# Experts of a mixture sorted by token count on chip, ten of them run with 64 slots in place of 96

## What is computed

```
def moe_ffn(h, w_router, b_router, w_up, b_up, w_down, b_down):
    logits = (t @ w_router + b_router)             # 512 tokens, 32 experts
    top_logit, top_e = lax.top_k(logits, TOP_K)    # TOP_K = 4
    gate = softmax(top_logit)
    ...
    def expert_block(args):                        # the tokens of one expert
        u = xb @ w_up[e] + b_up[e]                 # 1024 x 2048, float32
        glu = minimum(u[:, :D_FF], 7.0)
        lin = clip(u[:, D_FF:], -7.0, 7.0)
        act = glu * sigmoid(1.702 * glu) * (lin + 1.0)
        return act @ w_down[e] + b_down[e]         # 1024 x 1024, float32
    ...                                            # times gate, added per token
x = x + moe_ffn(rms_norm(x, norm_ffn_g), ...)
return rms_norm(x, norm_final_g)
```

## Time and profile before

| | |
|---|---|
| time, median of 3 runs | 1681.96 us (1681.91 to 1682.42) |
| the profiled execution | 1681.41 us, its span 1679.6 us |
| PE busy | 1625.1 us, 97% of the span |
| DVE, ACT, POOL busy | 541.3, 264.3, 211.1 us |
| read from HBM over the span | 456.51 MB |
| granted clock of PE, mean | 0.986 of full speed |

### The profile page before, as it was taken

The page is one execution under the profiler, slowest core; times in us unless marked ns, Lnnn a source line. Parts: engine busy times, 40 slices in busy tenths (PEclk is TensorE's granted clock), DMA queues, the critical chain, the costliest instruction groups (busy, mean ns, idle before and its releaser), DMA issues.

```text
span 1679.6 us, 31609 instructions
## 1 busy us (share of the span) xinstructions
PE 1625.1 (97%) x12295; PEld 743.6 (44%) x12296; DVE 541.3 (32%) x1449; ACT 264.3 (16%) x583; POOL 211.1 (13%) x205
## 2 busy tenths in 40 slices
PE   7999899999998899999999999999999999999994
PEld 3444465545545244444444444444444444444442
DVE  3224345321224523332242223322243223322232
ACT  3022333301211001110011101110011101111012
POOL 1000000150010111112111121112111121111111
PEclk9999999999998999999999999999999999999997
DMA  6211031141115799999999999999999999999995
GB/s 228 100 50 51 12 139 50 33 163 50 51 51 201 277 367 390 384 380 364 364 402 382 372 373 384 388 383 365 375 393 383 379 381 377 387 389 371 377 387 174
DMA packets 105493, 467.27 MB, mean 278 GB/s; under 512 B 14098, under 2 KB 14150, under 8 KB 72592
## 3 DMA queue, kind: packets, MB, share of 16 engines
q1 hardware_dynamic: 91768, 441.58, 66.8%
q0 software_dynamic: 13616, 25.19, 6.3%
q10 hardware_dynamic: 72, 0.02, 0.0%
HBM read 456.51 MB, written 18.87 MB: 283 GB/s over the span
## 4 chain that ended last, share of the span: by engine, by line
PE 95%; DVE 2%; ACT 1%; DMA 1%; issue 1%; ACTq 0%; POOLq 0%; POOL 0%; DVEq 0%
PE bank L735 40%; PE bank L687 23%; PE bank L763 13%; PE bank L772 6%; PE bank L724 1%; PE bank L703 1%; PE bank L713 1%; PE bank L925 1%; PE bank L908 1%; PE bank L705 1%; PE bank L716 1%; PE bank L951 1%; PE bank L750 1%; PE bank L796 1%; PE bank L852 1%
## 5 line engine op out<-in xcount | busy, mean ns | idle before, releaser
L735 PE MATMUL bank<-ring,arena 128*32 128x512 f32 x6144 | 679.3, 594 | 0.0
L735 PEld LDWEIGHTS bank<-ring,arena 128*32 128x32 f32 x6144 | 227.9, 110 | 400.0 <-issue 332.9
L763 PE MATMUL bank<-ring,arena 128*32 128x512 f32 x2048 | 267.8, 592 | 0.0
L687 PE MATMUL bank<-ring,actT 128*128 128x512 f32 x448 | 198.8, 599 | 0.1
L1579 DVE TENSOR_SCALAR tokA<-bank 64x512 f32<-64x512 f32 x64 | 43.7, 683 | 419.8 <-PE bank L735 418.7
L772 PE MATMUL bank<-ring,arena 128*32 128x512 f32 x1024 | 157.9, 592 | 0.0
L763 PEld LDWEIGHTS bank<-ring,arena 128*32 128x32 f32 x2048 | 112.9, 110 | 96.2
L593 POOL DMA_INDIRECT arena<-h_rows,arena x32 | 34.1, 1065 | 910.8 <-DVE arena L1563 853.6
L687 PEld LDWEIGHTS bank<-ring,actT 128*128 128x128 f32 x448 | 84.5, 193 | 98.8 <-issue 98.1
L1203 ACT ACTIVATE tokA<-tokA 128x512 f32<-128x512 f32 x32 | 20.1, 629 | 505.6 <-DVE tokA L1579 505.6
L687 PE MATMUL bank<-actT,ring 128*128 128x512 f32 x192 | 83.5, 593 | 0.0
(11 more groups left out here) (305 smaller groups left out, 1340.6 us busy)
## 6 DMA issues: line engine op xcount, KB each, us to landing
ring<-in_w_up SPq DMA_DIRECT2D x256, 1024.0 KB, 6.3
ring<-in_w_down SPq DMA_DIRECT2D x128, 1024.0 KB, 7.8
ring<-in_w_in SPq DMA_DIRECT2D x12, 1024.0 KB, 7.8
ring<-in_w_ck SPq DMA_DIRECT2D x4, 1024.0 KB, 6.2
ring<-in_w_out SPq DMA_DIRECT2D x4, 1024.0 KB, 6.2
ring<-in_w_cv SPq DMA_DIRECT2D x4, 1024.0 KB
ring<-in_w_cq SPq DMA_DIRECT2D x4, 1024.0 KB, 6.2
ring<-in_w_co SPq DMA_DIRECT2D x4, 1024.0 KB, 6.2
```

The costliest lines, as they stand in the source:

```text
L687: mm = pe.matmul(o, lhsT, rhs, start=(k == 0), stop=(k == KT - 1))
L735: mm = pe.matmul(bank[g][32 * t:32 * t + 32, :], lhsT, w[:, 512 * t:512 * t + 512], start=False, stop=(k == KT - 1))
L763: mm = pe.matmul(bank[3][r:r + 32, :], hTA[:, k % 4, g, k // 4, :], w[:, 512 * t:512 * t + 512], start=False, stop=(k == KT - 1))
```

## The change

**Order.** DVE counts the tokens of each expert, ranks the experts by count (a comparison of all 32 with all 32, on all partitions) and turns the ranks into `order_i`, the expert of each run. Runs 0 and 1 stay experts 0 and 1 (`tie` puts them last in rank). Runs 2, 3, 5, 6, 8, 9 and so on take the twenty largest of the rest, runs 4, 7, 10, ..., 31 the ten smallest. SP reads the expert of each transfer from `order_i` into a register, twice for each run (`expert_of`), DVE once for each run.

**Width.** A run `r` has `r.wide` false for the ten runs 4, 7, ..., 31. For these the work of group B is left out on all engines: matmuls, transposes, swiglu, gather, scatter. The threshold for a further run is 64 tokens for them (`over64`), 96 for the others. The loops are written for three runs at a time (wide, narrow, wide), with runs 0 to 2 ahead of the loop and 30 and 31 behind it. The dummy run 32, whose index and gather the kernel before still did, is gone.

**Overflow list.** It moves on DVE from ahead of `swiglu` of run 0 to behind the whole first iteration; its table has room for 31 in place of 22 entries, and three small operations go ahead of it.

**End.** The gather's and scatter's B parts have semaphores of their own. POOL reads the number of further runs ahead of the last scatter. SP in place of POOL reloads `x_res`. The squares of blocks 1 and 3 are taken by DVE, those of 0 and 2 by ACT.

```diff
+class Run:
+    def __init__(self, n, turn=None):
+        self.n, self.turn = n, turn
+        self.wide = n < 4 or n % 3 != 1
...
-            with sp_.Fori(0, NE - 1) as i:
-                load_up(i, UP_CHUNKS, i + 1)
-                load_down(i, UP_CHUNKS + UP_CHUNKS, i)
+            with sp_.Fori(2, LAST) as i:
+                load_up(i, UP_CHUNKS, expert_of(i + 1))
+                load_down(i, UP_CHUNKS + UP_CHUNKS, expert_of(i))
...
+            sp_.wait_ge(all_added, 1)
+            for b in range(NB):
+                sp_.dma_start(x_res[:, b, :], acc_full[P * b:P * b + P, :]).then_inc(fin_in[b], 16)
...
-                    for g in range(3):
+                    for g in range(3 if r.wide else 2):
                         lhsT = xTA[:, k % 4, g, k // 4, :] if g < 2 else xTB[:, k % 4, k // 4, :]
                         for t in range(4):
                             mm = pe.matmul(bank[g][32 * t:32 * t + 32, :], lhsT, w[:, 512 * t:512 * t + 512],
                                            start=False, stop=(k == KT - 1))
...
             for b in range(NB):
-                a.wait_ge(fin_in[b], 16)
-                squares(x_res[:, b, :], ss[:, b:b + 1], junk)
+                if b % 2 == 0:
+                    a.wait_ge(fin_in[b], 16)
+                    squares(x_res[:, b, :], ss[:, b:b + 1], junk)
+                else:
+                    a.wait_ge(fin_ss, b // 2 + 1)
                 rsqrt_mean(rstd[:, b:b + 1], ss[:, b:b + 1], D, fin_rstd)
...
+            own(v.scalar_tensor_tensor(out=key, in0=count_f[:, :], scalar=float(NE), in1=tie[:, :], op0=ALU.mult, op1=ALU.add))
+            own(v.tensor_tensor(pbuf_sq, key.unsqueeze(1).broadcast_to([P, NE, NE]),
+                                key.unsqueeze(2).broadcast_to([P, NE, NE]), ALU.is_gt))
+            own(v.tensor_reduce(rank_e, pbuf_sq, AX.X, ALU.add))
...
-                select_up(i + 1, i + 1)
-                slots_of(i + 2, i + 2, 0)
+                if not first:
+                    select_up(r + 1, part_of_run(r + 1))
+                if more:
+                    e = v.value_load(order_i[0:1, bass.ds(r.times(1, 2), 1)], min_val=0, max_val=NE - 1)
+                    slots_of((r + 2).wide, e, 0)
...
+            final_square(1)
+            final_scale(0)
+            final_square(3)
+            for b in (1, 2, 3):
+                final_scale(b)
```

More of the change, by code:

```diff
@@ L620, in _ @@
             g.wait_ge(xgT_done, 2)
[L621 to L628 removed]
+            gather(Run(2))
+            for n in range(1, LOOP_FROM):
+                gather_and_scatter(Run(n))
+            with g.Fori(0, LOOP_TURNS) as turn:
+                for u in range(3):
+                    gather_and_scatter(Run(LOOP_FROM + u, turn))
@@ L1004, in _ @@
+            for n in range(LOOP_FROM):
+                iteration(Run(n))
+            with pe.Fori(0, LOOP_TURNS) as turn:
+                for u in range(3):
+                    iteration(Run(LOOP_FROM + u, turn))
+            iteration(Run(LAST - 1), more=False)
+            hidden_T(Run(LAST))
+            down(Run(LAST), Run(LAST), UP_CHUNKS)
             pe.wait_ge(table_ready, 1)
@@ new lines, in iteration @@
+            def iteration(r, more=True):
+                results(r + -1, r + -1, 2 * UP_CHUNKS)
+                hidden_out_A(r)
+                gates(r + 1)
+                if more:
+                    rows_out_A(r + 2)
+            a.sem_inc(yA_ready, 1)
+            rows_out_A(Run(1))
+            gates(Run(0))
+            hidden_out_A(Run(0))
+            gates(Run(1))
+            rows_out_A(Run(2))
+            for n in range(1, LOOP_FROM):
+                iteration(Run(n))
+            with a.Fori(0, LOOP_TURNS) as turn:
+                for u in range(3):
+                    iteration(Run(LOOP_FROM + u, turn))
@@ L1578, in swiglu, with part_of_run @@
+            def part_of_run(r):
+                return part_run[:, bass.ds(r.times(1), 1)]
+            def swiglu(r, q, o, rows):
+                if r.wide:
+                    v.wait_ge(up_full, r.wides())
+                else:
+                    expert_chunks_used(v, q, o + UP_CHUNKS)
                 for g in range(2):
@@ new lines, in _ @@
+            rows_out_B(Run(1))
+            swiglu(Run(0), Run(0), 0, None)
+            iteration(Run(0), first=True)
+            overflow_table()
+            for n in range(1, LOOP_FROM):
+                iteration(Run(n))
+            ahead, moe.n, each = moe.n, 0, 0
+            with v.Fori(0, LOOP_TURNS) as turn:
+                moe.base = turn * 13 + ahead
+                for u in range(3):
+                    iteration(Run(LOOP_FROM + u, turn))
+                assert moe.n == 13
+            moe.base, moe.n = LOOP_TURNS * 13 + ahead, 0
```

590 lines of the change are left out of this document (339 added, 251 removed).

## The result

| | before | after |
|---|---|---|
| time, median | 1681.97 us (1681.91 to 1682.42, 4 runs) | 1638.24 us (1635.93 to 1640.40, 4 runs) |
| ratio, 95% interval | | 0.9739 (0.9722 to 0.9756) |
| profiled execution, its span | 1681.41, 1679.6 us | 1640.40, 1638.6 us |
| PE busy | 1625.1 us, 97% | 1530.5 us, 93% |
| granted clock of PE, mean | 0.986 | 0.979 |

What follows compares the result with a forecast made beforehand. The prediction took PE to bound the kernel, the DMA a close second and the loop's bound after the change: 30.8 + 4 + 9.5 - 5.8 + 1.3 = 39.8 us off 1681.41, 1641.6 us (range 1618 to 1672).

Steps and rivals of the forecast that it cites:

- PE-bound becomes DMA-bound: Expert loop: three runs want 91.8 us of PE but 100.1 us of DMA, so the DMA becomes the bound.
- The room of the DMA: Expert loop: the DMA could do an expert 1.1 us faster, 30.8 us over 28 iterations (22 to 48).
- The B gather and scatter: Narrow runs drop them: 0.4 us for each of ten runs, 4 us gained (0 to 8).
- The end of the expert stage: After the last weight landing: the result comes 2.2 us behind it, 9.5 us gained (8 to 10).
- The sort: On DVE, ahead of its wait for PE's transposes: 7.9 us of work with 2.6 us of cover left, cost nothing.
- The overflow list: Behind iteration 0: PE waits 4 us for the selection of run 2, plus 1.8 us of slower clock: 5.8 us lost.
- The tail: After the last result: B scatter 1.9 and register load 0.8 gained, split squares 1.3 lost: 1.3 us gained (-1 to 3).
- SP's waits for PE: Sign in the expert loop: if the forecast is right, SP's waits for PE to release chunks are gone.
- A (no room): Rival in the expert loop: the DMA has no room at all, 10.6 us gained, 1671 us; chance 0.12.
- B: Rival in the expert loop: the DMA has far more room and PE stays the bound, 1570 us; chance 0.04.
- C: Rival in narrow runs: PE's clock falls and the kernel gets slower, about 1799 us; chance 0.05.
- D: Rival in SP's queue: the new register loads are exposed, 37.5 us, about 1679 us, no change; chance 0.04.

Runs made afterwards that it cites:

- run 0: Not a follow-up kernel: the kernel's own pass for expert 0, ahead of the loop and wide.
- run 1: Not a follow-up kernel: the kernel's own pass for expert 1, wide; its bias matmuls come 30.0 us behind those of run 0, before 29.5.
- run 2: Not a follow-up kernel: the kernel's own wide pass for one of the twenty largest remaining experts; bias matmuls 39.66 us behind those of run 1, before 36.06.
- run 4: Not a follow-up kernel: the kernel's first narrow pass, for one of the ten smallest experts; its bias matmuls start 3.4 us later than before.
- pe_straight: The changed kernel with PE's loop written out for all iterations, the other engines keeping their loops: 1628.74 us, ratio to before 0.9691.
- narrow_all: All loops of the changed kernel written out and every run from the fifth on narrow, tokens beyond the 64th left out, all weights still loaded: 1616.34 us.
- grouped: Against all_straight, the ten narrow runs come last (22 to 31) and not every third: 1655.19 us.
- list_moved: Against pe_straight, DVE makes the overflow list inside iteration 0, ahead of its wait for PE: 1623.17 us.
- wide_straight: The changed kernel with every run wide and PE's loop written out: 1684.59 us, ratio to before 1.0019.
- more_loads: Against pe_straight, each register load in SP's queue is five, eight more for each expert: 1629.66 us.
- all_straight: The changed kernel with the loops of PE, ACT, DVE and GpSimd all written out, the order of runs kept: 1627.22 us.

## Why the prediction was right, and where it was not

**PE-bound becomes DMA-bound: right.** pe_straight, narrow_all and grouped show it from three sides: PE's work may fall by 169 us and the time by only 12; the DMA share is 1.02; and with the wide runs in a row PE's own pace of 34.44 us comes back. The period of three runs was to be 99 to 101 us and is 99.1. That it fell into this range is in part luck: two errors, told next, had opposite signs.

**Its size was wrong twice.** *The room of the DMA* was taken as 1.1 us an expert, the hole of the earlier trace rows filled up to 358 GB/s. Without the stops a wide run costs the DMA 32.75 us, so there were 34.47 - 32.75 = 1.7 us, just the value by the rate of 415 GB/s, which stood there as the upper end. My reading is that the hole is no place where gathers and scatters must fall; once the DMA is behind, the weights of the free stretches fill it. Over 28 iterations that is 48 us for 30.8. *The B gather and scatter* were worth 32.75 - 32.1 = 0.65 us for each narrow run, 6 to 7 us for 4. *The stop at the jump back* was in no term and no rival. It took back 9.5 us. The text listed the code "written for three runs at a time" and asked of every moved instruction what it costs, but not of the loop itself.

**The account** by the spans, before against after: start of run 4's bias matmuls 3.4 us later; run 4 to 31 38.3 us less; from there to the result 6.4 us less; from the result to the end 0.3 us more: 41.0 us. For pe_straight it is -3.2 + 52.1 + 6.0 + 0.6, 55.4 us by the spans.

In the prediction's own terms the account goes by the last landing of weights: 1645.7 us before, 1612.9 in the changed kernel, 1599.4 in pe_straight. So loop and list together gained 32.8 us, where 30.8 + 4 - 5.8 = 29.0 were predicted; the end of the stage gained 8.5 and the tail lost 0.3. In pe_straight loop and list gained 46.3 us. The sizes just given make more, 48 + 6.5 - 3.6 = 51 us, so 1.7 us for each expert is on the high side. The spans are read at PE's marks, and PE may have made up a part of its lag on the DMA between runs 4 and 31; the two were not taken apart.

**The end of the expert stage** worked as told: the result 2.1 us behind the last landing (2.2 predicted). The gain is 10.6 - 2.1 = 8.5 us and not 9.5: the 12.0 us before took the shortest landing of a down chunk, 5.4 us, and the last one took 6.8.

**The sort: right.** It ran from 558.64 to 566.2 us, DVE then still waited 2.75 us for PE (2.6 predicted). A rest of 0.5 us is there all the same: run 1's bias matmuls come 30.0 us behind run 0's, before 29.5. Its cause is open.

**The overflow list: the place right, the size not.** The wait is 3.6 us (36.06 to 39.66 between the bias matmuls), close to the 4 predicted, but there is no loss of clock behind it in the changed kernel's trace, for which I had added 1.8 us from the earlier trace rows. Two of the eleven traces with this wait have that loss, 1.7 us, so the term was possible and not certain. And "nothing of it comes back" was too hard, see list_moved. wide_straight puts all these small parts together at 2 to 3 us where the prediction had 4.5, or 6.4 without the 1.9 us for the B scatter of the last run, which wide_straight keeps.

**The tail** was to gain 1.3 us and lost 0.3 in this execution. The terms were near: the split costs 1 to 2 us (1.3 predicted), and what the B scatter and the register load gave is 23.3 - 21.4 = 1.9 us (2.7 predicted). On top of it the later blocks of the reload landed late here: DVE waited 1.88 us for block 3, where it was to work without a pause.

**Register loads: right**, eight more cost nothing. **SP's waits for PE were to be gone: wrong.** They are there in the changed kernel as before, since a full ring makes SP wait for a free slot whether PE or the DMA is behind; this sign can't tell the two apart, and PE's waits for landings can.

**Smaller points.** That PE falls up to 8 us behind in two wide runs has no working; by the prices found it is 2 x (34.47 - 32.75) = 3.4 us, and what follows from it holds. The forecast's own range reached down to 1615 us, the stated one to 1618.

**Rivals.** A (no room) is out with 405 GB/s held over 800 us; B, C and D are out by narrow_all and more_loads. The clock did fall in the changed kernel, but behind the stops and not behind waits for weights.

## What to carry to other kernels

When two engines are close, work taken from the first is paid only up to the second's pace: price the second from a stretch where it is saturated, and spread the saving so that the buffer between them evens it out (28 us here between the same runs in turns and in a row). When a loop's body grows, ask what its jump back costs. Look for waits called "issue" at the first instruction of the body and at the bytes of the instruction queue; writing the loop out took 9.5 us off where the DMA was the bound and 29 us where PE was. An earlier start of a stage that is bound by something else seems to be worth only part of itself.

## What the runs showed of the hardware that was not expected

- PE stands 2.3 to 3.9 us at the jump back of a body of three iterations (some 880 to 1000 matmuls and as many weight loads, as the profile counts them), and not at that of a body of one; in written-out code it doesn't stand. At each of 23 stops one 16 KB packet of the instruction queue is moved, and PE goes on 1.6 to 1.8 us behind its end.
- Behind a stop of 3.6 us PE's granted clock was 0.57 for 4 us, a mix of 1.2 and 2.4 GHz. It is not settled by the length alone: it fell behind one stop of 2.75 us and stayed at 1.00 behind one of 3.76 us, and behind the same wait of 3.1 us it fell in two traces of eleven. In narrow_all, with PE busy 77% of the time and no wait for weights over 2.1 us, the clock was 1.00.
- The DMA held 404 (all_straight) to 408 GB/s (narrow_all) from 700 to 1500 us, with gathers and scatters in it.
- Four blocks of 512 KB, issued within 1.8 us, were taken up by their readers 3.3, 4.7, 7.7 and 9.0 us behind the first issue in the changed kernel.
